# A transformer step's prompt forgetting attention: heads scored in pairs by 64-row products, bias and mask added on leaving PSUM, the V products alternated, the loops unrolled

## What is computed

```python
c_all = lax.cumsum(lf_all, axis=1)                      # (B, L, heads)
s = jnp.einsum('bqhd,bkhd->bhqk', qi, k) * D ** -0.5    # 128 queries at a time
s = s + ci.transpose(0, 2, 1)[..., None] - ckT          # bias[t, s] = c_t - c_s
s = jnp.where(kpos[None, :] <= qpos[:, None], s, -inf)
p = jax.nn.softmax(s, axis=-1)
o = jnp.einsum('bhqk,bkhd->bqhd', p, v)
```

## Time and profile before

| | us |
|---|---|
| median of 3 runs | 3962.7 (3962.61 to 3963.39) |
| span of the profiled execution, first to last instruction | 3952.7 |
| PE busy | 3552.3 (90%) |
| DVE, ACT, POOL busy | 943.0, 609.2, 904.9 |
| prompt forgetting attention, within the span | from 1580 to 1891 |

### The profile page before, as it was taken

How to read it: one execution, slowest core, us unless ns; L and a number is a source line. 1 busy time by engine, 2 the same in 40 slices (tenths; PEclk the granted TensorE clock), 3 DMA queues, 4 the chain that set the end, 5 groups by cost and what they waited for, 6 DMA issues and landing times. The chain is left out here.

```text
span 3952.7 us, 62014 instructions
## 1 busy us (share of the span) xinstructions
PE 3552.3 (90%) x23491; PEld 3160.2 (80%) x23491; DVE 943.0 (24%) x1363; ACT 609.2 (15%) x987; POOL 904.9 (23%) x946
## 2 busy tenths in 40 slices
PE   6999999996977986999488887999988899999996
PEld 5999999995966985566355555888887899999995
DVE  2111111124053115334233332111133211111114
ACT  3000000002011013222143442000012200000002
POOL 1233232221200210100224333111111222332220
PEclk8999999998987998789688888999999899999998
DMA  4111111101111122000499996111110111111111
GB/s 133 37 50 45 35 50 48 37 27 32 32 36 41 42 62 86 1 0 0 81 278 331 308 310 207 41 40 40 40 29 19 37 48 37 43 51 39 40 39 52
DMA packets 318955, 286.93 MB, mean 73 GB/s; under 512 B 28913, under 2 KB 258546, under 8 KB 318834
## 3 DMA queue, kind: packets, MB, share of 16 engines
q1 hardware_dynamic: 292946, 208.67, 17.6%
q0 software_dynamic: 25888, 76.63, 6.9%
HBM read 272.95 MB, written 12.22 MB: 72 GB/s over the span
## 5 line engine op out<-in xcount | busy, mean ns | idle before, releaser
L563 DVE TENSOR_TENSOR hid<-silu,f_acc 128x1092 f32<-128x1092 f32 x44 | 56.9, 1293 | 904.2 <-PE f_acc L203 904.2
L203 PE MATMUL f_acc<-x_hi,w_hi_last 128*128 128x364 f32 x1056 | 233.2, 329 | 27.5 <-SPq L481 27.5
L203 PE MATMUL f_acc<-x_hi,w_hi_first 128*128 128x364 f32 x1056 | 234.5, 330 | 7.0 <-SPq L481 7.0
L203 PE MATMUL f_acc<-x_hi,w_lo_last 128*128 128x364 f32 x1056 | 233.9, 330 | 0.0
L203 PE MATMUL f_acc<-x_lo,w_hi_first 128*128 128x364 f32 x1056 | 233.7, 329 | 0.0
L203 PE MATMUL f_acc<-x_hi,w_lo_first 128*128 128x364 f32 x1056 | 233.7, 329 | 0.0
L203 PE MATMUL f_acc<-x_lo,w_hi_last 128*128 128x364 f32 x1056 | 233.5, 329 | 0.0
L2114 PE MATMUL d_ktp<-ident_sb,d_k_in 128*128 128x128 f32 x1024 | 184.0, 312 | 48.9 <-DMA d_k_in<-cache_fox_k 35.2
L161 POOL CAST w_hi_first<-w_raw_first 128x1024 fp32r<-128x1024 f32 (+2 forms) x92 | 73.4, 798 | 630.8 <-PE f_acc L203 290.6
L161 POOL CAST w_hi_last<-w_raw_last 128x1024 fp32r<-128x1024 f32 (+2 forms) x92 | 73.4, 798 | 610.6 <-PE f_acc L203 605.8
L203 PEld LDWEIGHTS f_acc<-x_hi,w_hi_last 128*128 128x128 f32 x1056 | 183.9, 189 | 28.1 <-issue 28.1
(11 more groups left out here) (345 smaller groups left out, 6587.4 us busy)
## 6 DMA issues: line engine op xcount, KB each, us to landing
d_k_in<-cache_fox_k SPq DMA_DIRECT2D x256, 256.0 KB, 8.0
d_v_in<-cache_fox_v POOLq DMA_DIRECT2D x256, 256.0 KB, 6.6
w_raw_mix<-w_in SPq DMA_DIRECT2D x24, 512.0 KB, 4.3
w_raw_first<-w_ffn_gate SPq DMA_DIRECT2D x22, 512.0 KB, 3.9
w_raw_first<-w_ffn_up SPq DMA_DIRECT2D x22, 512.0 KB, 3.8
w_raw_last<-w_ffn_gate SPq DMA_DIRECT2D x22, 512.0 KB, 3.8
w_raw_last<-w_ffn_up SPq DMA_DIRECT2D x22, 512.0 KB, 3.9
w_raw_first<-w_ffn_down SPq DMA_DIRECT2D x40, 256.0 KB, 2.8
```

The source lines that it names most:

```text
L203: mm = self.nc.tensor.matmul(out[:, b, 0:width], w[s][:, k, :], x[:, k, b * width:(b + 1) * width], start=(k == 0 and first), stop=(k == k ...
L563: nc.vector.tensor_tensor(blocks_of(hid[:]), blocks_of(silu[:]), acc[1][:, :, 0:TB], ALU.mult).then_inc(free[1], 1)
```

## The change

The score of a head is a product over its own 64 rows, straight from `g.br` and `g.fkv`, and the two heads of a pair are issued in turn, 512 keys at a time (L1761). There is no zeroed copy of the queries, no bias product, no mask product and no copy of V; `p_own`, `p_sel`, `p_neg_hi` and `p_neg_lo` are gone. Instead -c_s goes to DRAM in an earlier phase (`neg_d`), and SP loads it back for each pair onto all 128 partitions (`p_bias`, 1 MB). POOL adds the mask to the last 128 columns of it (`p_on_diag`, `corner`). DVE reads the scores from PSUM, adds bias, writes the sum to SBUF (`p_s`) and takes the maximum in one operation (`tensor_tensor_reduce`, L1855, and L1867 for the last 128 keys). ACT takes the exponential in place in SBUF. The unit is now both heads of a query block (n, 32 of them); turned squares of one head go to `p_ptp0`, of the other to `p_ptp1`, in pieces of at most 4 blocks of keys; ACT empties the one, DVE the other. V products alternate between the heads, that is between the two 64-column halves of the array (L1788). The diagonal matrix is made by POOL. The loop over pairs is written out.

```diff
@@ phase_attention_in
-def phase_attention_in(g):
+def phase_attention_in(g, neg_d):
...
-        gb = g.negc
+        gb = g.sb(ctx, "gb", [H_F, TW])
...
+                sp.wait_ge(scanned, 1)
+                sp.dma_start(neg_d, gb[:, 0:TP]).then_inc(stored, 16)
                 sp.wait_ge(nat, 1)
...
-                sp.wait_ge(stored, 32)
+                sp.wait_ge(stored, 48)
@@ phase_fox_prompt
+    pieces = [(n, x) for n in range(UNITS) for x in range(2 if block_of(n) >= HALF else 1)]
+    first = [pieces.index((n, 0)) for n in range(UNITS)] + [len(pieces)]
     with ExitStack() as ctx:
+        s_buf = [g.sb(ctx, f"p_s{e}", [P, 2, TP]) for e in range(2)]
+        bias = [g.sb(ctx, f"p_bias{e}", [P, 2, TP]) for e in range(2)]
+        on_diag = [g.sb(ctx, f"p_on_diag{e}", [P, 2, P]) for e in range(2)]
+        pt = [g.mem_kt[:].rearrange("p a (b k) -> p (a b) k", k=P).rearrange("p (s b) k -> p s b k", s=2),
+              g.mem_v[:].rearrange("p a (b k) -> p (a b) k", k=P).rearrange("p (s b) k -> p s b k", s=2)]
...
+                for p in range(PAIRS):
+                    if p >= 2:
+                        sp.wait_ge(taken, 2 * NCH * (p - 1))
+                    src = neg_d[2 * p:2 * p + 2, :].unsqueeze(0).broadcast_to([P, 2, TP])
+                    sp.dma_start(bias[p % 2][:], src).then_inc(bias_ok[p % 2], 16)
...
+                def corner(n):
+                    p, i, e = n // NCH, block_of(n), n % 2
+                    pool.wait_ge(bias_ok[p % 2], 16 * (p // 2 + 1))
+                    if n >= 2:
+                        pool.wait_ge(taken, 2 * (n - 1))
+                    nc.gpsimd.tensor_tensor(on_diag[e][:], bias[p % 2][:, :, i * P:(i + 1) * P],
+                                            g.causal[:].unsqueeze(1).broadcast_to([P, 2, P]), ALU.add)\
+                        .then_inc(diag_bias, 1)
+                def diagonal(n):
+                    e = n % 2
+                    pool.wait_ge(recip, n + 1)
+                    if n >= 2:
+                        pool.wait_ge(spread_ok, 2 * (n - 1))
+                    nc.gpsimd.tensor_tensor(diag[e][:], g.ident[:].unsqueeze(1).broadcast_to([P, 2, P]),
+                                            rsum[e][:].unsqueeze(2).broadcast_to([P, 2, P]), ALU.mult)\
+                        .then_inc(diag_ok, 1)
+                corner(0)
+                corner(1)
+                for n in range(UNITS):
+                    diagonal(n)
+                    if n + 2 < UNITS:
+                        corner(n + 2)
...
-                        for k0 in range(0, keys, 512):
-                            k1 = min(k0 + 512, keys)
-                            out = sc[s][:, k0:k1]
-                            nc.tensor.matmul(out, qz[:, s, i * P:keys], g.fkv[:, p, k0:k1], start=True, stop=False)
-                            nc.tensor.matmul(out, sel[:, s, :], neg_hi[:, k0:k1], start=False, stop=False)
-                            nc.tensor.matmul(out, sel[:, s, :], neg_lo[:, k0:k1], start=False, stop=(k1 < keys))
-                        nc.tensor.matmul(sc[s][:, i * P:keys], ident[:], causal[:], start=False, stop=True)\
-                            .then_inc(scored, 1)
...
+                def scores(n):
+                    p, i, keys = n // NCH, block_of(n), keys_of(n)
+                    if n > 0:
+                        pe.wait_ge(taken, 2 * n)
+                    for k0 in range(0, keys, 512):
+                        k1 = min(k0 + 512, keys)
+                        for s, rows in enumerate(HALVES):
+                            mm = nc.tensor.matmul(sc[s][:, k0:k1], g.br[rows, 8 + p, i * P:keys], g.fkv[rows, p, k0:k1],
+                                                  start=True, stop=True)
+                            if k1 == keys:
+                                mm.then_inc(scored, 1)
+                def turn(piece):
+                    n, x = pieces[piece]
+                    e, i = n % 2, block_of(n)
+                    pe.wait_ge(exped, 2 * n + 2)
+                    for s in range(2):
+                        if piece > 0:
+                            pe.wait_ge(pt_ok[s], piece)
+                        for k in range(x * HALF, min(i + 1, (x + 1) * HALF)):
+                            mm = nc.tensor.transpose(ptp[s][:, k - x * HALF, :], s_buf[e][:, s, k * P:(k + 1) * P], g.ident[:])
+                        mm.then_inc(turned, 1)
+                def products(piece):
+                    n, x = pieces[piece]
+                    p, e, i = n // NCH, n % 2, block_of(n)
+                    for s in range(2):
+                        pe.wait_ge(pt_ok[s], piece + 1)
+                    if x == 0 and n >= 2:
+                        pe.wait_ge(o_read, n - 1)
+                    last = min(i + 1, (x + 1) * HALF) - 1
+                    for k in range(x * HALF, last + 1):
+                        for s, rows in enumerate(HALVES):
+                            v = g.fkv[:, 4 + p, k * P + s * DF:k * P + (s + 1) * DF]
+                            mm = nc.tensor.matmul(out[e][rows, 0, :], v, pt[piece % 2][:, s, k - x * HALF, :],
+                                                  start=(k == 0), stop=(k == i))
+                            if k == last:
+                                mm.then_inc(valued, 1)
+                    if last == i:
+                        pe.wait_ge(diag_ok, n + 1)
+                        for s, rows in enumerate(HALVES):
+                            nc.tensor.matmul(out[e][rows, 1, :], g.ones[:, 0:DF], diag[e][:, s, :], start=True, stop=True)\
+                                .then_inc(spread_ok, 1)
+                scores(0)
+                scores(1)
+                for piece, (n, x) in enumerate(pieces):
+                    turn(piece)
+                    if piece > 0:
+                        products(piece - 1)
+                    if piece + 1 == first[n + 1] and n + 2 < UNITS:
+                        scores(n + 2)
+                products(len(pieces) - 1)
...
+                def exps(n):
+                    e, keys = n % 2, keys_of(n)
+                    if n >= 2:
+                        act.wait_ge(recip, n - 1)
+                    for s in range(2):
+                        act.wait_ge(taken, 2 * n + s + 1)
+                        nc.scalar.activation(s_buf[e][:, s, 0:keys], s_buf[e][:, s, 0:keys], ACT.Exp,
+                                             bias=nmax[e][:, s, 1:2], scale=-1.0, accum_out=ssum[e][:, s:s + 1])\
+                            .then_inc(exped, 1)
+                def place(piece):
+                    n, x = pieces[piece]
+                    k = min(block_of(n) + 1 - x * HALF, HALF)
+                    act.wait_ge(turned, 2 * piece + 1)
+                    if piece >= 2:
+                        act.wait_ge(valued, 2 * (piece - 1))
+                    nc.scalar.copy(pt[piece % 2][:, 0, 0:k, :], ptp[0][:, 0:k, :]).then_inc(pt_ok[0], 1)
+                def inverse(n):
+                    act.wait_ge(spread_ok, 2 * n + 2)
+                    if n >= 1:
+                        act.wait_ge(o_read, n)
+                    nc.scalar.copy(inv[:], out[n % 2][:, 1, :]).then_inc(inv_ok, 1)
+                exps(0)
+                for piece, (n, x) in enumerate(pieces):
+                    place(piece)
+                    if x == 0 and n + 1 < UNITS:
+                        exps(n + 1)
+                    if x == 0 and n > 0:
+                        inverse(n - 1)
+                inverse(UNITS - 1)
...
+                    dve.wait_ge(bias_ok[p % 2], 16 * (p // 2 + 1))
+                    if n >= 2:
+                        dve.wait_ge(turned, 2 * first[n - 1])
+                    if i > 0:
+                        for s in range(2):
+                            dve.wait_ge(scored, 2 * n + s + 1)
+                            nc.vector.tensor_tensor_reduce(s_buf[e][:, s, 0:i * P], sc[s][:, 0:i * P], bias[p % 2][:, s, 0:i * P],
+                                                           -1.0, 3e38, ALU.add, ALU.min, nmax[e][:, s, 0:1])\
                                 .then_inc(maxed, 1)
+                    dve.wait_ge(diag_bias, n + 1)
+                    done = 2 * (n - n // NCH)
+                    for s in range(2):
+                        start = 3e38
+                        if i > 0:
+                            dve.wait_ge(maxed, done + s + 1)
+                            start = nmax[e][:, s, 0:1]
+                        else:
+                            dve.wait_ge(scored, 2 * n + s + 1)
+                        nc.vector.tensor_tensor_reduce(s_buf[e][:, s, i * P:keys], sc[s][:, i * P:keys], on_diag[e][:, s, :],
+                                                       -1.0, start, ALU.add, ALU.min, nmax[e][:, s, 1:2])\
+                            .then_inc(taken, 1)
...
+                fused(0)
+                fused(1)
+                for piece, (n, x) in enumerate(pieces):
+                    if x == 0:
+                        invert(n)
```

(43 more changed lines are left out.)

135 lines of the change are left out of this document (13 added, 122 removed).

## The result

The changed kernel takes 3796.15 us (median of 4 runs, 3789.45 to 3797.45), the one before 3963.05 in the same comparison: a ratio of 0.9582, 95% interval 0.9558 to 0.9607. The phase lasts from 1577.6 to 1728.5, 150.8 us where it was 310.6, and everything outside it together 3643.6 where it was 3642.2. So what the span lost (158.3 us) is all in the phase, and the phase beat the sum (195) by 44 us.

What follows compares the result with a forecast made beforehand. PE was taken to bound the kernel, afterwards a PE-DVE ring: 7 + 153 + 1 = 161 us, plus 34 for low clock, a 195 us phase, 116 less; span 3837 plus 10.0 gave 3847 us, range 3818 to 3900.

Steps and rivals of the forecast that it cites:

- the sum: Attention of the prompt: 161 us at full clock plus 34 for low clock, 195 us for the phase.
- What bounds the kernel, and what is late next: Prompt attention: PE bound before; afterwards a chain through PE and DVE, 38.3 us a pair, PE busy 80%.
- a ring of DVE and PE: Middle steps of a pair: PE and DVE wait for each other in turn, 3.35 + 0.587k us for k blocks.
- The prices on PE: PE's scores, squares, V products and diagonals, rows and columns paired: together 30.6 us a pair, where a pair took 77.
- S(6): Both heads' scores over 6 blocks on PE, row halves side by side: 0.2 + 0.21 per block, forecast 1.46 us.
- Rivals 1 and 5: Score row halves run one after the other: 3877 us, chance 0.14; products start strictly in program order: 3858, chance 0.05.
- The price on DVE: DVE's new operation, two per head: 0.133 us per block, 0.158 fixed and 0.1 read-out per operation.
- F: DVE's two operations per head, for both heads of a unit: 0.27 us per block plus 1.03.
- Rival 3: DVE's new operation takes two cycles per element: 2 us on 896 elements, not about 1.1; chance not in the text.
- The clock: Phase at half clock for the first 30 us and 20 at each boundary, 90 us in all: 34 us more.
- Ends: Start and end of the phase: DVE starts about 7 us in, 5 earlier than before; 1 us at the end.
- The time around the span: Whole program: 10.0 us between span and median, taking the span of 3837 to 3847 us.

Runs made afterwards that it cites:

- the run on the same rows: Changed kernel with both heads' scores made from rows 0 to 63: phase 170.4 us, median 3816.8 us.
- its control: Kernel before with only PE's loop over pairs written out: phase 300.2 us, median 3960.9 us, ratio 1.0005 to before.
- V in a row: Changed kernel with all V products of a piece for head 0, then all for head 1: phase 163.3 us, median 3810.0 us.
- scores head by head: Changed kernel with all score products of one head issued before the other's: phase 152.6 us, median 3798.9 us.
- one DVE operation twice: Changed kernel with POOL adding the mask in place, one DVE operation per head, run twice: phases 145.3 and 145.0 us, medians 3789.7 and 3791.1 us.
- the unpaired kernel: Changed kernel with both heads' scores from rows 0 to 63 and V products not alternated: phase 184.9 us, median 3828.7 us.

## Why the prediction was right and wrong

- **What bounds the kernel, and what is late next**: right. PE bounded the phase; now a ring of DVE and PE, with PE busy for 88% of it after the start. A pair takes 35.84 us (1620.45 to 1656.29 on DVE) where the sum said 38.3; its eight steps, from 8 blocks to one, take 3.53, 5.14, 6.15, 5.86, 5.26, 4.68, 2.74 and 2.47 us, forecast 3.6, 5.1, 6.87, 6.28, 5.70, 5.11, 2.7 and 2.9.
- **The prices on PE**: right. S(6) 1.49 for 1.46, V 0.055 a record, squares 0.109 for 0.107. Side-by-side row halves, for which no row spoke, are shown by the run on the same rows. Rivals 1 and 5 are false.
- **The price on DVE**: mis-sized, by the read-out and the fixed part. F of 6 blocks is 2.03 us (1595.92 to 1597.95), forecast 2.65. What a unit costs beyond its elements is 0.43 us, not 1.03: the operation with the bias (L1855) takes 0.08 us beyond its elements at every width, the one on the last 128 keys (L1867) 0.14, where I had 0.26 for both, and the read-out's 82 ns lie mostly over the next operation. Rival 3 is false: 1089 ns for 896 elements. The Trainium skill's about 75 ns per instruction ("Vector Engine (DVE) Microarchitecture Reference", "5.2 Measured stream behaviour on trn2") was nearer than my value from ACT's read-out: by it, as an estimate, the part beyond the elements would be 0.6. Of the 0.6 us that F gave, the middle steps kept 0.4 to 0.7; the handover from PE's scores to DVE alone took 0.24 us (1595.68 to 1595.92) where I had 0.05. The four middle steps are 2.0 us a pair, the last step 0.4, together 2.5 a pair and 10 in all.
- **The clock**: this is the step that failed. "The first 30 us and 20 at each boundary, 90 us", for +34, was carried over from the kernel before. It was 12.3 us, at the start only, and 18.5 in the second profile. In the first, 5.6 of the 12.3 had passed before DVE could start, and DVE's first pair took 37.19 us (1583.26 to 1620.45), 1.35 more than its second: that is about what the low clock cost. I had read the falls as the answer to thin steps and less cover. The case without low clock at the boundaries stood in the prediction only as the low end, 157 us and 3809, outside the range, and the phase of 150.8 us is under the 165 named as a sign of being wrong. The runs show two parts.
  - Whether it falls: every fall at a boundary began during a wait of PE or within about 2 us of its end. With the wait taken out of the kernel before there was none at three boundaries. With waits of 1.6 to 1.8 us it fell at 3 of 6 in the kernel before and its control, and at 5 of 6 in the two with no 8-row products or with widened ones; with waits of 3.4 us at 3 of 3. The changed kernel did not lose this wait, as said above: with 1.4 to 1.7 us the clock fell at 4 of 18 boundaries (both its profiles, V in a row, scores head by head, one DVE operation twice), so its first profile without a fall is in part luck. Such a wait makes a fall possible, not certain.
  - How long it stays low: with products of 8 rows among those of 128, 13.7, 23.9 and 17.1 us at a boundary; without them 3.4 us in all nine falls behind waits of 1.4 to 1.8 us, and 3.4 to 6.8 in the two runs with other waits (3.4 us added, and 0.85 in the unpaired kernel). At the start, behind a wait of some 7 us in every variant of the kernel before, 29.3, 29.2 and 21.8 us with them, 9.9 without, 10.5 with all of them on 128 rows; in the changed kernel and its variants 10 to 19.

  So what the change took away is the mix of 8 and 128 rows, not the wait. The term is 1.35 us where I had 34: 32.6 of the 44 us. Two falls of 3.4 us, as in the second profile (153.9 us), would have left it some 3 us higher.
- **Ends**: DVE started at 5.6 us, not 7, and the last pair took 0.5 us more to its last output, not 1: 1.9 us. Writing PE's loop out cost nothing, as said, in the kernel before; in the changed one no run tests it.
- **The time around the span**: I took median minus span, 10 us, as constant. Every run here for which both are given has 1.6 to 2.0 us around its span. So the profiled execution of before took about 3954 us, some 8 us under the median. Much of the spread sits in the attention of the samples: 492.6 to 513.7 us in the fourteen profiles, in which that phase is the same code. It is 496.6 in that of before, so where its own 8 us lie isn't shown.
- The sum: clock 32.6, ring 9.8, ends 1.9, the mistaken 8, less 1.4 elsewhere: 51 us, from 3847 to 3796. Without the mistaken 8 the forecast would have been 3839 and the range would still have begun at 3810: the miss is the clock's.
- **Where the 159.8 us came from**: changes between 8 and 128 rows and the clock that goes with them 58.2 (310.6 to 252.4; 64 in the medians of the same rounds), what the bias and mask products cost otherwise 36.2 (to 216.2), the pairing of rows and columns 34.1 (184.9 to 150.8). The 31.3 between 216.2 and 184.9 are one kernel's structure against the other's. Of them about 3 are shorter waits of PE at the boundaries (5.3 us against 2.5), and 2.5 DVE's earlier start (5.7 us against 8.2); that the rest is diagonal products for two heads at once and one fixed part of 0.2 us for both heads' scores is argued from rows, not shown by a run of its own.

## What to carry to other kernels

Before pricing a clock, find what made it fall in the kernel at hand, and what kept it low: here a wait and a mix of row counts. The change removed the second only, and the low time at the boundaries went from 14 to 24 us a fall to 3.4 or none. A product with few rows among products with many costs more than its columns: 0.2 us at each change here, so pad it with zero rows or move it to another engine. Compare a span with other runs' spans, not a span with a median, and take a second profile before reading a fall of the clock, or its absence, as the kernel's own.

## What was not expected of the hardware

Adding 120 zero rows to 192 small products made the phase 58 us faster with no other edit. In V products issued one head after the other the second head still started early: 0.087 us a record, between the 0.055 of alternation and 0.11 alone. And behind the same wait of about 1.7 us the clock fell at some boundaries of an execution and not at others.
